# Head squares behind the scan's copies, and filter transform products ahead of the squares' sums

## The chip, the cores and the metric

The kernel runs on one core of a Trainium2 chip. The metric is the device time of one execution in microseconds (us). Engines are named as in the profile: PE is TensorE's matmul side and PEld its weight loads, DVE is VectorE, ACT is ScalarE, POOL is GpSimd, SP is SyncE. L1624 is line 1624 of the kernel before.

## The reference, cut to what matters

One inference step of a hybrid backbone on 128 context tokens and 512 latent tokens, width 1024, all in float32. Three pieces of it are touched: the filters of the long convolution, the modulated norm in front of the mixer, and the head norm and output projection at its end.

```python
def hyena_filters(seq_len, p):                 # for 128 and for 512 positions
    ...
    h = (h @ w3 + b3).reshape(seq_len, HY_ORDER, 2, HY_WIDTH)
    window = exp(-t * abs(decay)) + HY_MOD_SHIFT
    h = h * window
    h = h * rsqrt(sum(h * h, axis=(0, 2)) + EPS)       # squares summed over positions and directions
    ...

def mixer(xm, p, state, grid):
    proj = xm @ w_in                           # q, k, v, o, gates, three hyena parts
    h_f, (cf, nf, mf) = mlstm_scan(...)        # forward
    h_b, (cb, nb, mb) = mlstm_scan(...)        # backward
    h = h_f + rev(h_b)
    h = h * rsqrt(mean(h * h, axis=-1) + EPS)          # per head
    y_ml = h * head_gain * sigmoid(o)
    z = parts[-1]
    for n in range(HY_ORDER):
        z = parts[n] * long_conv(z, filt[n, 0], filt[n, 1], hy_bias[n])   # FFT of the filter
    return concatenate([y_ml, z]) @ w_out

h = rms_norm(x, g_norm) * (1 + sc) + sh        # sh, sc from silu(c) @ w_ada + b_ada
y = mixer(h, ...)
x = x + g1 * rms_norm(y, g)
x = x + g2 * rms_norm(hier_moe(rms_norm(x, g) * (1 + sc2) + sh2), g)      # 16 experts, top 2
```

## The kernel before

All of it is one program with an order written out by hand for every engine; the engines meet only through named counting semaphores. A helper `link` makes each VectorE or ScalarE operation bump a semaphore and wait for itself, so work on these engines runs strictly in the order written. A wait at the head of a queue holds everything behind it.

**Filters.** For each of two orders `o`, TensorE makes ten filter blocks (five 128-position tiles t, two directions s; w = 2t + s). ScalarE makes the window (`win`), VectorE multiplies it in (L973) into `ab`, ScalarE squares the block (`square`, L647), and VectorE turns the two directions of a tile into sum and difference (`combine`, L964 and L965). TensorE sums the squares over positions in three batches (`sum_squares`, L1596), the last behind block 9. Pieces of the modulation product (`ada_piece`, L1558) are strewn in between; each uses one 2 MB chunk of weights in a ring of three slots.

Then come ten transform products g per order (L1624, for g of 8 and 9 L1620): product 0 reads tile 1, product 1 tile 2, products 2 and 3 tiles 3 and 4. They go round four PSUM banks. ScalarE copies out products 0, 4, 5, 6, 8, 9 (`spectrum`, L655), VectorE adds out 1, 2, 3, 7 (L1000, L1001). Product 4 needs the bank of product 0, product 5 that of 1, product 7 that of 3. Between them lie: ScalarE's copy of the summed squares (L666), TensorE's lane sums (L1630), ScalarE's two square roots (L674), which need a table load, and on VectorE the bias rows (L984, L986: four operations of one row), which product 7 needs. In the second order TensorE also turns the first third of the modulation (`ada_turn(0)`, L1572) and does `ada_piece(7)` behind product 4.

**First norm.** ScalarE squares the five tiles of x (`x_square`, L622) in between, takes the root (L680), VectorE the reciprocal `xrs` (L994), and ScalarE scales the five tiles of `x_raw` in place (L686), between its copies of products 4, 5, 6. TensorE waits for all five and transposes x in ten bank-fuls (L1645), two in flight per evicting engine: even ones go to ScalarE (L699, L703), odd ones to VectorE (L1024, L1028), which apply `scaleA` and `mod` on the way to `hT`. Those two come from `ada_columns(0)` (L1013) and L1017, which VectorE does behind the cosine halves (L1003, L1004) of the second order. Then TensorE goes on with `ada_piece(8)` (L1558) and the projections.

**Scan.** Ten steps i, alternating direction. TensorE per step: half an output gate product (`out_gate_half`, L1803), the product with the state (L1848), with the values (L1856), and for the first eight the state update (L1864). ScalarE copies the state product out in four (L829) and, in odd steps, the output gate (`out_gate`, L783). VectorE adds the values' product to it (L1281). From step 7 on the first heads are normed: VectorE `heads_sum` (h_ready), ScalarE `heads_square` (L796), VectorE `heads_squares` (L1246), ScalarE `heads_root` (L800, with a table load), VectorE `heads_norm`.

**Output projection.** For each of five tiles j: `out_hyena` (L1888, 16 instructions per tile), `turn_heads` (TensorE L1873, VectorE L1301), `out_mlstm` (L1898, 16), then VectorE's `residual` into `x2` (L1314 to L1320) and TensorE's transposes of `x2` (L1908). The rows that `residual` needs and x itself are loaded by POOL when the last sum of the scan is done; `residual(0)` waits for x_sample.

**Experts.** Routing, then up to 70 groups of 32 token slots; the weights of expert e + 3 are loaded into the slots of expert e when its products are done.

Of the kernel before, what the change touches and what calls it, by code (L numbers as in the profile page):

```python
# [9 lines left out]
ALU = mybir.AluOpType  # L10
# [93 lines left out]
def emit(nc, a, stack):  # L104
# [491 lines left out]
    def _(act):  # L596
# [61 lines left out]
        for w in range(20):  # L658
            o = w // 10
            if w % 10 != 9:  # L660
                win(w + 1)
            square(w)
            if w % 10 == 9:
                act.wait_ge(S["sq_done"], 3 * o + 3)
                for i, rows in enumerate((P, 2 * LANE)):
                    link(A(lane_sums[i], ps[0:rows, 5 + i, :], ACT.Copy), "lanes_read")  # L666
                spectrum(o, 0)
                for t in ((0,), (2, 3))[o]:
                    x_square(t)
                act.wait_ge(S["norm_done"], o + 1)  # L670
                if o:
                    act.wait_ge(S["norm_stored"], 32)
                for i in range(2):
                    link(A(norm_rows[i], ps[0:1, 5 + i, :], ACT.Sqrt, bias=epsc[0:1, :]), "norm_sqrt")  # L674
                if o == 0:
                    win(w + 1)
                    x_square(1)
                else:
                    x_square(4)
                    link(A(xss, xss, ACT.Sqrt, bias=epsc, scale=1.0 / D), "x_rstd")  # L680
                for g in (4, 5, 6, 8, 9):
                    spectrum(o, g)
                    if o and g < 8:
                        act.wait_ge(S["xrs_ready"], 1)
                        for t in {4: (0, 1, 2), 5: (3,), 6: (4,)}[g]:
                            link(A(x_raw[:, t, :], x_raw[:, t, :], ACT.Copy, scale=xrs[:, t:t + 1]), "xn_ready")  # L686
            if w == 10:
                ada_row(0)
# [132 lines left out]
        for i in range(NSTEP):  # L821
# [3 lines left out]
            if t:  # L825
                act.wait_ge(S["inter_done"], i - 1)
                for h in range(H):
                    b, c = half4(h)
                    link(A(num[t][:, H * d + h, :], ps[:, 4 + b, c:c + DH + 1], ACT.Copy,  # L829
                           scale=qcols[:, t, 1, 32 * d + h:32 * d + h + 1]), "inter_read" if h == 3 else "act_chain")  # L830
            if i in (7, 8):
                heads_square(i - 7)

# [101 lines left out]
    def _(dve):  # L935
# [23 lines left out]
        link(CP(gate_pick[:, :, 32:32 + H], folded[:, 2:4, :]))  # L959

        def combine(o, t):

            dve.wait_ge(S["sq_ready"], 10 * o + 2 * t + 2)
            link(TT(ab[:, 1, t, :], ab[:, 1, t, :], ab[:, 0, t, :], ALU.subtract))  # L964
            link(STT(ab[:, 0, t, :], ab[:, 0, t, :], 2.0, ab[:, 1, t, :], ALU.mult, ALU.add),  # L965
                 "comb_done" if t == NT - 1 else "dve_chain")

        for o in range(ORD):
# [20 lines left out]
            for g in BY_VECTOR:  # L989
                if g == 3:  # L990
                    bias_rows_in()
                if o and g == 3:
                    dve.wait_ge(S["x_rstd"], 1)
                    link(dve.reciprocal(xrs, xss), "xrs_ready")  # L994
                n = 20 * o + 10 + g
                dve.wait_ge(S["filt_done"], n + 1)
# [4 lines left out]
                link(TT(h[:, old, :], new, h[:, old, :], ALU.subtract), "filt_read")  # L1001
            h = spec_h[:, o, 0]
            link(TT(h[:, 0:4:2, :], h[:, 0:4:2, :], h[:, 1:4:2, :], ALU.add))  # L1003
            link(STT(h[:, 1:4:2, :], h[:, 1:4:2, :], -2.0, h[:, 0:4:2, :], ALU.mult, ALU.add))  # L1004


        def ada_columns(third):

            dve.wait_ge(S["ada_t"], third + 1)
            lo = 16 * third  # L1010
            src = ps[:, ADA_BANK[third], :].rearrange("p (b j q) -> p j b q", b=4, j=4)[:, :, :, 0:2]
            bias = colsT[:, lo:lo + 16].rearrange("p (j b) -> p j b", j=4).unsqueeze(3).broadcast_to((P, 4, 4, 2))
            return link(TT(mod[:, lo:lo + 16, :].rearrange("p (j b) g -> p j b g", j=4), src, bias, ALU.add),  # L1013
                        "mod_ready")

        ada_columns(0)
        link(STT(scaleA, mod[:, 8:16, :], 1.0, colsT[:, 48:56].unsqueeze(2).broadcast_to((P, 8, 2)),  # L1017
                 ALU.add, ALU.mult), "modA_ready")
        for n in range(1, 10, 2):
# [73 lines left out]
        def context_products(o):  # L1093
# [10 lines left out]
            link(TT(xs, p[2], p[3], ALU.subtract), "mul_done")  # L1104

        dve.wait_ge(S["norm_cols"], 32)
        link(dve.reciprocal(norm_columns, norm_columns))
# [419 lines left out]
    def _(pe):  # L1527
# [72 lines left out]
        for o in range(ORD):  # L1600
            for w in range(10):
# [7 lines left out]
                if w in piece:  # L1609
                    ada_piece(4 * o + piece.index(w))  # L1610
            sum_squares(o, 2)
            pe.wait_ge(S["comb_done"], o + 1)
            pe.wait_ge(S["ld_dft"], 32)
            for g in range(10):
                n = 20 * o + 10 + g
                b = filter_bank(n)
                if g == 7:
# [8 lines left out]
                mm.then_inc(S["filt_done"], 1)  # L1626
                if g == 0:
                    pe.wait_ge(S["lanes_read"], 2 * o + 2)
# [8 lines left out]
        pe.wait_ge(S["spec_read"], 12)  # L1637
        pe.wait_ge(S["xn_ready"], NT)
        for n in range(10):
# [294 lines left out]
        out_hyena(0)  # L1934
        out_hyena(1)
        pe.wait_ge(S["st_ready"], LAST_UPD)
        turn_heads(0)
        out_mlstm(0)
        turn_heads(1)
        out_mlstm(1)  # L1940
# [118 lines left out]
```

## Time and profile before

| what | value |
|---|---|
| median of 3 runs | 868.31 us (863.45 to 868.75) |
| time of the profiled execution | 864.98 us |
| its span, first to last instruction | 862.1 us |
| mean granted TensorE clock | 0.967 |
| PE busy | 778.7 us (90%) |
| DVE, ACT, POOL busy | 49%, 33%, 13% |
| DMA | 191.40 MB, mean 222 GB/s |

```profile
PE   4998799999999999999998999799999989899920
PEclk9999999999999999989999999799999999999975
DMA  8978451132044402133009516969999999999145
```

The three strips cut the span in 40 equal slices of 21.55 us, with tenths of busy share, granted clock and DMA share. The filters fill the slices 2 to 5, the scan ends in slice 21, the experts run from slice 27 to 38.

### The profile page before, as it was taken

How to read it: one execution, taken by the hardware profiler on the slowest of the kernel's cores; microseconds unless marked ns; L12 is line 12 of the kernel's file. 1: busy time of each engine (PE TensorE's matmuls, PEld its weight loads, DVE VectorE, ACT ScalarE, POOL GpSimd, SP SyncE). 2: the span in 40 equal slices, each digit the busy share in tenths (PEclk: the TensorE clock that was granted, in tenths of full speed). 3: DMA queues.
4: the chain of work that ended last, by engine and by line, in shares of the span. 5: the costliest groups of instructions: out<-in, count | busy, mean ns of one | idle time of the engine just before them, and what ended most of it. 6: DMA issues, size and time to landing. Idle time of an engine off the chain costs nothing.

```text
span 862.1 us, 16880 instructions
## 1 busy us (share of the span) xinstructions
PE 778.7 (90%) x6727; PEld 448.2 (52%) x6727; DVE 419.9 (49%) x761; ACT 281.2 (33%) x559; POOL 108.5 (13%) x211
## 2 busy tenths in 40 slices
PE   4998799999999999999998999799999989899920
PEld 1232455554554457456664444357777667566610
DVE  5566713225881681754554675733343333243428
ACT  1667702113101201256222333223333333233315
POOL 4000100000001000001002000122222222122231
PEclk9999999999999999989999999799999999999975
DMA  8978451132044402133009516969999999999145
GB/s 246 411 300 341 134 195 36 63 114 82 18 178 165 132 1 99 25 123 123 0 22 367 202 44 221 397 244 418 416 420 416 419 418 420 419 415 393 61 150 233
DMA packets 40681, 191.40 MB, mean 222 GB/s; under 512 B 4641, under 2 KB 4937, under 8 KB 33010
## 3 DMA queue, kind: packets, MB, share of 16 engines
q1 hardware_dynamic: 29434, 155.12, 45.5%
q0 software_dynamic: 8640, 29.00, 9.9%
q10 hardware_dynamic: 2552, 6.50, 2.1%
q8 instruction: 41, 0.67, 0.3%
q14 instruction: 14, 0.11, 0.0%
HBM read 174.15 MB, written 16.45 MB: 221 GB/s over the span
## 4 chain that ended last, share of the span: by engine, by line
PE 73%; DMA 12%; DVE 7%; issue 3%; ACT 3%; SPq 1%; POOL 0%; POOLq 0%; DVEq 0%; ACTq 0%
PE banks L1654 16%; PE banks L2003 14%; DMA arena<-in_w_up 8%; PE banks L2014 6%; PE banks L1794 4%; PE banks L1655 4%; PE banks L1898 4%; PE banks L1888 4%; PE banks L1803 3%; DMA arena<-in_w_ada 3%; PE banks L1624 2%; PE banks L1686 2%; PE banks L1759 2%; PE banks L1558 2%; PE banks L1604 1%
## 5 line engine op out<-in xcount | busy, mean ns | idle before, releaser
L2003 PE MATMUL banks<-arena 128*32 128x256 f32 x3072 | 177.1, 382 | 9.0 <-DMA arena<-in_w_up 7.9
L1654 PE MATMUL banks<-arena 128*128 128x512 f32 x320 | 164.2, 595 | 1.5 <-issue 0.8
L2003 PEld LDWEIGHTS banks<-arena 128*32 128x32 f32 x3072 | 115.2, 111 | 63.0 <-issue 12.7
L1655 PEld LDWEIGHTS banks<-arena 128*128 128x128 f32 x320 | 60.8, 190 | 76.5 <-issue 76.5
L1480 DVE STREAM_TRANSPOSE arena<-arena 128x256 f32<-128x256 f32 x49 | 32.3, 659 | 135.3 <-PE banks L2003 130.1
L2014 PE MATMUL banks<-arena 128*32 128x256 f32 x1536 | 92.7, 379 | 1.2 <-DVE arena L1504 1.2
L2014 PEld LDWEIGHTS banks<-arena 128*32 128x32 f32 x1536 | 57.6, 110 | 26.7 <-DVE arena L1504 1.7
L1655 PE MATMUL banks<-arena 128*128 128x128 f32 x320 | 61.5, 274 | 0.0
L893 ACT ACTIVATE arena<-banks 32x256 f32<-32x256 f32 x98 | 36.7, 374 | 71.3 <-PE banks L2014 70.7
L1487 DVE COPY arena<-banks 32x256 f32<-32x256 f32 x98 | 41.4, 422 | 33.2 <-PE banks L2014 32.5
L1654 PEld LDWEIGHTS banks<-arena 128*128 128x128 f32 x320 | 48.5, 192 | 4.8 <-issue 3.3
L564 POOL DMA_INDIRECT arena<-expert_input,arena x47 | 46.3, 984 | 12.5 <-issue 12.5
L1042 DVE SCALAR_TENSOR_TENSOR arena<-banks,arena 128x504 f32<-128x504 f32 x12 | 8.9, 743 | 72.5 <-ACT arena L718 72.5
L912 ACT ACTIVATE arena<-banks 128x128 f32<-128x128 f32 x48 | 13.4, 278 | 92.1 <-PE banks L2003 92.1
L717 ACT ACTIVATE arena<-banks,arena 128x512 f32<-128x512 f32 x12 | 8.2, 687 | 97.9 <-PE banks L1655 97.9
L909 ACT ACT_TABLE_LOAD x24 | 30.8, 1283 | 28.6 <-DVE arena L1487 22.1
L1794 PE MATMUL banks<-arena 128*128 128x512 f32 x80 | 37.7, 633 | 0.0
L1888 PE MATMUL banks<-arena 128*128 128x512 f32 x80 | 35.1, 593 | 2.5 <-ACT arena L783 2.5
L1898 PE MATMUL banks<-arena 128*128 128x512 f32 x80 | 35.6, 598 | 1.7 <-DVE arena L1301 1.7
L1803 PE MATMUL banks<-arena 128*128 128x512 f32 x80 | 36.1, 594 | 0.0
L561 POOL COPY arena<-arena 128x1 int32 x47 | 8.5, 181 | 176.2 <-DVE arena L1480 176.2
L1794 PEld LDWEIGHTS banks<-arena 128*128 128x128 f32 x80 | 16.1, 204 | 20.2 <-issue 20.2
(378 smaller groups left out, 985.5 us busy)
## 6 DMA issues: line engine op xcount, KB each, us to landing
arena<-in_w_down SPq DMA_DIRECT2D x16, 2048.0 KB, 31.1
arena<-in_w_gate SPq DMA_DIRECT2D x15, 2048.0 KB, 26.7
arena<-in_w_up SPq DMA_DIRECT2D x15, 2048.0 KB, 31.7
arena<-in_w_ada SPq DMA_DIRECT2D x12, 2048.0 KB, 13.6
arena<-in_w_in SPq DMA_DIRECT2D x7, 2048.0 KB, 7.7
expert_output<-arena ACTq DMA_DIRECT2D x49, 128.0 KB, 6.5
expert_output<-arena POOLq DMA_DIRECT2D x1, 4096.0 KB, 20.4
arena<-in_w_out SPq DMA_DIRECT2D x2, 2048.0 KB, 7.9
```

The lines of the kernel that those rows point to most:

```text
L564: pool.indirect_dma_start(xr[n], None, h2_quarters, bass.IndirectOffsetOnAxis(ap=idx_now[n], axis=0))\
L893: ins = act.activation(ysb[n][:, l * 256:(l + 1) * 256], ps[l * LANE:(l + 1) * LANE, 5, 0:256], ACT.Copy)
L1480: dve.transpose(xg, xr[n].rearrange("p (r k) -> p k r", k=KD)).then_inc(S["xg_ready"], 1)
L1487: ins = dve.tensor_copy(ysb[n][:, l * 256:(l + 1) * 256], ps[l * LANE:(l + 1) * LANE, 5, 0:256])
L1654: M(ps[:, b, :], lhs, hT[:, k, CTX:TOK], start=k == 0, stop=k == KD - 1)
L1655: mm = M(ps[:, b + 1, 0:CTX], lhs, hT[:, k, 0:CTX], start=k == 0, stop=k == KD - 1)
L1794: mm = M(ps[:, 1 + n % 4, :], hT[:, k, n * P:(n + 1) * P], w[:, k, :], start=k == 0, stop=k == KD - 1)
L1803: mm = M(ps[:, 1, :], hT[:, k, t * P:(t + 1) * P], w[:, k, :], start=k == 0, stop=k == KD - 1)
L1888: M(ps[:, 1 + 2 * (j % 2) + c, :], part1t[:, k, t * P:(t + 1) * P], w[:, NB + k, :], start=k == 0, stop=False)
L1898: mm = M(ps[:, 1 + 2 * (j % 2) + c, :], ymlT[:, k, t * P:(t + 1) * P], w[:, k, :], start=False, stop=k == NB - 1)
L2003: mm = M(ps[q * LANE:(q + 1) * LANE, 2, 0:2 * P].rearrange("p (g a j) -> p g a j", g=2, j=LANE), xg[:, k, :], gate_up[e % 3][:, :, k, q, : ...
L2014: mm = M(ps[l * LANE:(l + 1) * LANE, 5, 0:256], aT[:, q * LANE:(q + 1) * LANE], downs[e % 3][:, q, l * 256:(l + 1) * 256], start=q == 0, s ...
```

## The change

Ahead of the last sum of squares of an order, TensorE now does transform products 0 and 1, each behind a `comb_done` of its own tile (`comb_done` now counts four per order). Product 2 follows the sum, and the lane sums follow product 2 (before: product 0). ScalarE copies product 0 before the summed squares. Of x's tiles ScalarE scales three (0, 1 behind product 4, 2 behind product 5); VectorE scales 3 and 4, ahead of its adds for product 7 of the second order, and right behind them does `ada_columns(0)` and `scaleA`. The cosine halves of the second order move behind VectorE's writes of `hT`. TensorE's wait ahead of the x transposes is for three scalings and for `modA_ready`. At the end of the scan `heads_square(0)` and `heads_square(1)` go one step back, behind the copies of steps 8 and 9, and TensorE does `turn_heads` 0 and 1 each behind one `out_hyena`, ahead of both `out_mlstm`.

```diff
@@ ScalarE, filters @@
             if w % 10 == 9:
+                spectrum(o, 0)
                 act.wait_ge(S["sq_done"], 3 * o + 3)
                 for i, rows in enumerate((P, 2 * LANE)):
                     link(A(lane_sums[i], ps[0:rows, 5 + i, :], ACT.Copy), "lanes_read")
-                spectrum(o, 0)
...
-                        for t in {4: (0, 1, 2), 5: (3,), 6: (4,)}[g]:
+                        for t in {4: (0, 1), 5: (2,), 6: ()}[g]:
@@ ScalarE, scan @@
-            if i in (7, 8):
-                heads_square(i - 7)
+            if i in (8, 9):
+                heads_square(i - 8)
@@ VectorE @@
-                 "comb_done" if t == NT - 1 else "dve_chain")
+                 "comb_done" if t else "dve_chain")
+        def cosine_halves(o):
+            h = spec_h[:, o, 0]
+            link(TT(h[:, 0:4:2, :], h[:, 0:4:2, :], h[:, 1:4:2, :], ALU.add))
+            link(STT(h[:, 1:4:2, :], h[:, 1:4:2, :], -2.0, h[:, 0:4:2, :], ALU.mult, ALU.add))
...
+                if o and g == 7:
+                    for t in (3, 4):
+                        link(TS(x_raw[:, t, :], x_raw[:, t, :], xrs[:, t:t + 1], None, ALU.mult))
+                    ada_columns(0)
+                    link(STT(scaleA, mod[:, 8:16, :], 1.0, colsT[:, 48:56].unsqueeze(2).broadcast_to((P, 8, 2)),
+                             ALU.add, ALU.mult), "modA_ready")
...
-            h = spec_h[:, o, 0]
-            link(TT(h[:, 0:4:2, :], ...))
-            link(STT(h[:, 1:4:2, :], ...))
-        ada_columns(0)
-        link(STT(scaleA, ...), "modA_ready")
+            if o == 0:
+                cosine_halves(o)
...
+        cosine_halves(1)
         dve.wait_ge(S["norm_cols"], 32)
@@ TensorE, filters @@
-            sum_squares(o, 2)
-            pe.wait_ge(S["comb_done"], o + 1)
             pe.wait_ge(S["ld_dft"], 32)
             for g in range(10):
                 n = 20 * o + 10 + g
+                if g == 2:
+                    sum_squares(o, 2)
+                if g < 3:
+                    pe.wait_ge(S["comb_done"], 4 * o + (1, 2, 4)[g])
...
-                if g == 0:
+                if g == 2:
                     pe.wait_ge(S["lanes_read"], 2 * o + 2)
...
-        pe.wait_ge(S["xn_ready"], NT)
+        pe.wait_ge(S["xn_ready"], 3)
+        pe.wait_ge(S["modA_ready"], 1)
@@ TensorE, output projection @@
         out_hyena(0)
-        out_hyena(1)
         pe.wait_ge(S["st_ready"], LAST_UPD)
         turn_heads(0)
+        out_hyena(1)
+        turn_heads(1)
         out_mlstm(0)
-        turn_heads(1)
         out_mlstm(1)
```

## Rows read from the trace of the kernel before

**Rows 1.** Busy time in stretches: length, engines busy (instructions), PEclk, DMA share, GB/s
```profile
450.90:478.20 27.30, 23.09 (x65) 10.87 (x65) 13.43 (x25) 6.89 (x15) 4.45 (x8) 1.00 0.96 364
...
380.00:385.00 5.00, 5.00 (x7) 1.89 (x6) 1.22 (x4) 4.64 (x12) 0.00 (x0) 0.50 0.00 0
...
580.00:800.00 220.00, 212.08 (x3888) 147.04 (x3881) 81.27 (x203) 71.31 (x162) 54.87 (x121) 0.99 1.00 413
```

**Rows 2.** Timeline, TensorE, filters: start, us, what, idle before and its releaser
```profile
42.89 1.06 PE L1596 MATMUL banks<-arena 128*32 128x512 f32 x8 [1.62 <-ACT arena L647]
...
45.08 1.13 PE L1624 MATMUL banks<-arena 128*128 128x512 f32 x2 [1.13 <-DVE arena L965]
...
46.14 1.97 PE L1630 MATMUL banks<-arena 128*1 128x512 f32 x4
...
48.03 9.83 PE L1624 MATMUL banks<-arena 128*128 128x512 f32 x22
...
80.32 1.13 PE L1624 MATMUL banks<-arena 128*128 128x512 f32 x2 [1.13 <-DVE arena L965]
```

**Rows 3.** Timeline, order 0: roots, bias rows, product 7's weight load; a later table load
```profile
48.19 1.28 ACT L674 ACT_TABLE_LOAD   x1
...
49.48 1.39 ACT L674 ACTIVATE arena<-banks,arena 1x512 f32<-1x512 f32 x2
...
52.42 1.39 DVE L984 TENSOR_TENSOR arena<-arena 1x512 f32<-1x512 f32 x2
...
56.74 0.30 PEld L1624 LDWEIGHTS banks<-arena 128*128 128x128 f32 x2 [0.68 <-DVE arena L1001]
...
547.67 1.28 ACT L882 ACT_TABLE_LOAD   x1 [6.45 <-DVE arena L1413]
```

**Rows 4.** Timeline, end of order 1, scaling and transposing of x
```profile
87.65 1.39 DVE L984 TENSOR_TENSOR arena<-arena 1x512 f32<-1x512 f32 x2
...
90.79 3.51 ACT L686 ACTIVATE arena<-arena 128x1024 f32<-128x1024 f32 x3 [0.55 <-DVE arena L994]
...
95.30 1.88 PE L1620 MATMUL banks<-arena 128*128 128x512 f32 x4
...
97.95 1.23 ACT L655 ACTIVATE arena<-banks 128x512 f32<-128x512 f32 x2
...
99.27 1.94 PE L1645 MATMUL banks<-arena 128*128 128x128 f32 x16 [2.09 <-ACT arena L655]
...
101.32 1.93 ACT L699 ACTIVATE arena<-banks,arena 128x128 f32<-128x128 f32 x4 [1.51 <-DVE arena L1017]
...
103.30 2.84 PE L1645 MATMUL banks<-arena 128*128 128x128 f32 x24 [2.09 <-ACT arena L699]
...
104.50 2.56 DVE L1028 TENSOR_SCALAR arena<-banks,arena 128x512 f32<-128x512 f32 x3 [0.64 <-PE banks L1645]
...
107.16 3.64 PE L1558 MATMUL banks<-arena 128*32 128x512 f32 x32 [1.02 <-ACT arena L703]
```

**Rows 5.** Timeline, end of the scan, output projection, first residual
```profile
444.61 1.05 PE L1848 MATMUL banks<-arena 128*128 128x129 f32 x8
...
446.70 0.63 ACT L796 ACTIVATE arena<-arena 128x512 f32<-128x512 f32 x1 [5.48 <-DVE arena L1242]
...
447.36 1.58 ACT L829 ACTIVATE arena<-banks,arena 128x129 f32<-128x129 f32 x4
...
454.29 13.97 PE L1888 MATMUL banks<-arena 128*128 128x512 f32 x32 [2.50 <-ACT arena L783]
...
469.55 7.13 PE L1898 MATMUL banks<-arena 128*128 128x512 f32 x16 [0.85 <-DVE arena L1301]
...
479.60 0.15 DVE L1314 TENSOR_SCALAR arena<-arena 128x1 f32<-128x1 f32 x1 [1.69 <-DMA arena<-in_x_sample]
...
482.75 0.69 DVE L1320 TENSOR_TENSOR arena<-arena 128x512 f32<-128x512 f32 x1
...
485.38 1.04 PE L1908 MATMUL banks<-arena 128*128 128x128 f32 x8
```

More of the change, by code:

```diff
@@ L959, in _, with ada_columns @@
         link(CP(gate_pick[:, :, 32:32 + H], folded[:, 2:4, :]))
+        def ada_columns(third):
+            dve.wait_ge(S["ada_t"], third + 1)
+            lo = 16 * third
+            src = ps[:, ADA_BANK[third], :].rearrange("p (b j q) -> p j b q", b=4, j=4)[:, :, :, 0:2]
+            bias = colsT[:, lo:lo + 16].rearrange("p (j b) -> p j b", j=4).unsqueeze(3).broadcast_to((P, 4, 4, 2))
+            return link(TT(mod[:, lo:lo + 16, :].rearrange("p (j b) g -> p j b g", j=4), src, bias, ALU.add),
+                        "mod_ready")
         def combine(o, t):
@@ L1001, in _ @@
                 link(TT(h[:, old, :], new, h[:, old, :], ALU.subtract), "filt_read")
-            h = spec_h[:, o, 0]
[L1003 to L1014, printed above, removed]
-        ada_columns(0)
-        link(STT(scaleA, mod[:, 8:16, :], 1.0, colsT[:, 48:56].unsqueeze(2).broadcast_to((P, 8, 2)),
-                 ALU.add, ALU.mult), "modA_ready")
+            if o == 0:
+                cosine_halves(o)
         for n in range(1, 10, 2):
```

## The prediction, made before the change was run

> **What bounds the kernel now.** I read the page first, for the shares, and then busy time by stretch: TensorE leads everywhere, as in the longest stretch shown, where it is busy for 212 of 220 us and no other engine for half of it [rows 1]. So only two kinds of time can be won: stretches in which TensorE stands still, and matmuls that run at half clock. Then I read the timeline of the two stretches that the diff touches.
>
> *Filters, first order.* TensorE is idle 1.62 us before the last squares' sum (it waits for ScalarE's last square) and 1.13 us before the first transform product (it waits for VectorE's last combine) [rows 2]. The second order repeats this. Behind it in the first stands a chain over three engines: lane sums, ScalarE's table load (1.28) and two roots (1.39), VectorE's four bias operations (one row of two, 1.39, stands for both), its adds for product 3, and then TensorE's product 7, which waited for those adds (its weight load starts at 56.74) [rows 3].
> *Between filters and the first projections.* TensorE starts the transposes of x at 99.27 after 2.09 us idle, starts the second batch at 103.30 after 2.09 more, and the modulation products at 107.16 [rows 4]. ScalarE carries this: five scalings of x at 1.16 us each, between copies of products at 0.60.
> *End of the scan.* ScalarE idles 5.48 us with heads_square(0) at the head of its queue, and only then does the four copies of step 8 (1.58); the same square sits ahead of step 9's copies. TensorE idles 2.50 us before the output projection, and 0.85 us twice, once behind each of the first two head transposes (the row of one is shown) [rows 5].
> From the projections to the scan, and in the expert stage, TensorE is close to gapless. In the expert stage the weight stream is full as well (DMA share 1.00 from 580 to 800), but its first load waits for expert 0's products, so the stream starts earlier if TensorE does [rows 1]. A gain ahead of it should pass through whole.
>
> **Part 1, order 0, on the clock of before.** TensorE is free at 42.89 - 1.62 = 41.27. Products 0 and 1 need only combines 1 and 2, which are long done. They are four instructions; a product instruction costs 0.43 (22 in 9.83, fill included) [rows 2], so they take 1.72 and end at 42.99: the squares' sum moves by 0.1 at most, and the combine still ends just before 45.08. There product 2 (four instructions) stands where product 0 (two) stood. Lane sums start at 46.14 + 0.86 = 47.00 and end at 48.97. Product 3 starts at 48.89 instead of 48.03 + 0.86 + 1.72 = 50.61, so TensorE is 1.72 ahead.
> But the lane sums end 0.86 later. Is the table load held by the wait? The load of line 882 stands behind 6.45 us of idling for VectorE [rows 3], so I take it that loads start after the wait. Then load 49.05, roots 50.34 to 51.73 (before: to 50.87). VectorE, which before only came to the bias rows at 52.42 because of its adds for product 2, is now free by 48.6 and waits for the roots: bias rows 51.77 to 54.58, adds for product 3 to 56.03, product 7 at 56.09 instead of 56.74. TensorE would have been there at 54.91. **0.65 of the 1.72 remains.** Bounds: 0, if another wait appears, and 1.72, if the roots are not late.
>
> **Order 1.** The same swap, still on the clock of before. Its product 0 started at 80.32, 35.24 after order 0's, so the lane sums end at 48.97 + 35.24 = 84.2, and load and roots at 86.95. Before, VectorE came to its bias rows at 87.65 [rows 4], later than the roots; now it comes at 87.0, so bias rows, x's reciprocal and ScalarE's scalings (90.79) are 0.65 sooner. ScalarE scales three tiles, not five: 2 x 1.18 = 2.36 less. Its last copy would end at 99.18 - 0.65 - 2.36 = 96.17, but product 9, with TensorE 1.72 ahead and no later wait, is on PSUM at 95.30 + 1.88 - 1.72 and a fill, 95.8, so this copy ends at 96.5. Transposes at 96.6 instead of 99.27: 2.67 won, with order 0's 0.65 **3.32**.
> VectorE now scales tiles 3 and 4 (two operations of 1024 elements, not in the trace: below by nothing, above by 2 x 0.69 each, the price per 512 elements of its adds [rows 3]; I take 0.7 to 1.4), then ada_columns and scaleA (0.2 each). All of it fits between the adds of product 3 (at 91.5) and those of product 7 (not before 95.0, ScalarE's copy of product 6); were the cover gone, it would cost up to 3.2. The modulation is then ready before the transposes. Before, ScalarE's first write of hT came at 101.32, 2.05 after the transposes began; now it needs only the first transposed bank, which by the row of the second batch (TensorE 103.30, VectorE's first write behind two banks at 104.50) is about 0.8: **1.26 more**. The rest up to 107.16 keeps its length [rows 4].
> The cosine halves (two operations, 2.5 us) move behind this, into VectorE's wait of 12 us for the first projection: nothing. The weight chunk for that projection is issued when modulation product 7 ends, and moves with it. Part 1: 3.32 + 1.26 = **4.6**.
>
> **Part 2, the scan's end.** Step 8's copies start when TensorE's product is there (445.7), not at 447.36. TensorE's own work in the scan ended at 454.29 - 2.50 = 451.79; two blocks of eight products (1.05 each) before that is the last output gate product, at about 450, so ScalarE's copy of it is done at 450.7, step 9's copies (behind the first of those blocks) at 452.6, and the second square follows them. The output projection's first half waits for the output gate (now 450.7) and its second for VectorE's last sum (453.4), so TensorE goes on at 451.64 instead of 454.29: **2.65**. The heads' chain (root with table load, norm 1.65) is ready at 456.6, ahead of the first half's end at 458.6; each transpose now has a projection of 7 us behind it, and both waits of 0.85 go: with the fills **1.85** [rows 5]. TensorE would reach the transposes of x2 4.5 ahead, at about 481.0.
> There something else is late: residual(0) waits for x_sample, released at 479.60. These loads go out on the last sum, 3.2 us sooner, but the queues were full from 450.9 to 478.2 but for 4% of 27.3 us [rows 1], and the first weights in them start as before. So it lands only 1.15 sooner. The second half of x2 is then ready at 482.75 + 0.69 - 1.15 = 482.3 against TensorE at 481.4: about 1.05 is given back. Part 2: 4.5 - 1.05 = **3.45**. VectorE's later residuals come 1.2 to 1.8 sooner, TensorE needs them 3.45 sooner, and they had 3.7 us to spare.
>
> **Sum:** 4.6 + 3.45 = 8.05. The profiled execution took 864.98 (span 862.1), the median is 868.31, 3.3 above. From the one I get 856.9, from the other 860.3; I predict the middle, 858.6.
>
> **Rivals.**
> *A: the roots are not late* (the table load runs ahead of the wait; line 882 speaks against it): 1.07 more in each order, 10.2 in all, 856.4. Chance 0.08.
> *B: the table switch costs more on the chain.* In these rows the root starts 0.01 after the load. If a switch after a wait took a second 1.28, both orders would lose it: 5.5 in all, 861.1. Chance 0.06. The Trainium skill (ScalarE: Activation LUTs, What ACT_TABLE_LOAD costs) puts a drain of 1.38 us beside the load's 1.28; by it the sum would be 8.05 - 2.76 = 5.3. The trace agrees on the load (1.28) and shows no drain behind it.
> *C: part 2 is eaten by x2.* x_sample lands no sooner, and TensorE waits for it a further 1.15: 6.9, 859.7. The full queues speak for it, the 4% of gaps against. Chance 0.12.
> *D: the clock moves.* From 380 to 385 the values' products ran at 0.50 (1.2 GHz), after a stretch of small transposes: 2.5 us lost, some 3 with the edges [rows 1]. If this fall goes, 855.5; if it doubles, 861.7. Nothing in the diff acts on it, but all of it shifts. Chance 0.17, both ways.
> *E: slower.* TensorE falls to 1.2 GHz among the x transposes (small products, as before 380) and stays there over the modulation products and first projections. An us at half clock loses 0.5, so it decides from 16 us on; at 18 us: 8.05 - 9 = 1 slower, 867.6. Before, this stretch had longer gaps and did not fall. Chance 0.02.
> The forecast itself: 0.55.
>
> **Numbers.** About 1% is what a measurement of this kernel can tell from no change. 8.05 is 0.93% of the profiled execution's time, so the forecast lies just inside that border and C further in: A, the good half of D and nearly half of the forecast (its terms are good to about 1 us) lie beyond it: faster 0.46, within 1% 0.51, slower 0.03. The three runs shown spread over 5.3 us, and that spread is wider than the rivals'; the range takes A and the good D below, B and the bad D above, from either base: 854.5 to 862.5.
>
> **What would show it.** Two more products between the last filter modulation product and the squares' sum in each order; product 7 still waiting for VectorE, some 1.2 us; the x transposes near 95.9 and the modulation products near 102.6; no gap of TensorE over 0.3 between scan and output projection, and one of about 1 us at the x2 transposes. I am wrong if VectorE's scalings take more than 1.7 each, if the table load starts ahead of the lane sums' end, or if the expert stage does not shift by the same 8 us.

## The result, and the profile after

| | before | after |
|---|---|---|
| median, us | 866.85 (863.45 to 868.75, 4 runs) | 854.34 (853.44 to 855.89, 4 runs) |
| ratio, 95% interval | 1 | 0.9865 (0.9842 to 0.9887) |
| profiled execution: time / span | 864.98 / 862.1 | 855.89 / 854.1 |
| mean granted clock | 0.967 | 0.967 |

The kernel became 1.35% faster, more than the 1% that a measurement can tell from no change. The forecast was 858.6; the measured 854.34 is 4.3 us under it and 0.16 under the low end of the range (854.5). The two profiled executions differ by 8.0 us in span and 9.1 in time, the medians by 12.5. The mechanisms are therefore read from the traces, and the difference between 8 and 12 is a question of its own.

In the changed kernel the line numbers have moved: the filter products are L1635, the lane sums L1641, the turns of the output projection L1885, its products L1900 and L1910, the transposes of x2 L1920.

**Filters, first order.** The timeline of the changed kernel, TensorE, then ScalarE, then VectorE (start, us, what, idle before and its releaser). Compare [rows 2, 3].

```profile
41.12 1.98 PE L1635 MATMUL banks<-arena 128*128 128x512 f32 x4
43.03 1.06 PE L1605 MATMUL banks<-arena 128*32 128x512 f32 x8
45.01 1.98 PE L1635 MATMUL banks<-arena 128*128 128x512 f32 x4 [0.91 <-DVE arena L974]
...
56.06 1.13 PE L1635 MATMUL banks<-arena 128*128 128x512 f32 x2 [0.97 <-DVE arena L1022]
...
48.97 1.28 ACT L674 ACT_TABLE_LOAD   x1 [2.34 <-PE banks L1641]
50.26 1.39 ACT L674 ACTIVATE arena<-banks,arena 1x512 f32<-1x512 f32 x2
...
51.74 1.39 DVE L999 TENSOR_TENSOR arena<-arena 1x512 f32<-1x512 f32 x2 [3.24 <-ACT arena L674]
53.17 1.40 DVE L1001 TENSOR_TENSOR arena<-arena 1x512 f32<-1x512 f32 x2
54.60 0.69 DVE L1021 TENSOR_TENSOR arena<-arena,banks 128x512 f32<-128x512 f32 x1
```

The first two products stand ahead of the squares' sums and fill the wait of 1.62; at product 2 TensorE still waits 0.91 for the last combine (before 1.13). The chain behind the lane sums then holds product 7: the table load waits for the lane sums (2.34 us idle ahead of it), the root starts 0.01 us behind the load, the four row operations follow, and TensorE waits 0.97.

**End of the second order.** The same timeline around the transposes of x (L1657) and the modulation products (L1567). Compare [rows 4].

```profile
90.88 1.54 DVE L1012 TENSOR_SCALAR arena<-arena 128x1024 f32<-128x1024 f32 x2
...
94.40 0.69 DVE L1021 TENSOR_TENSOR arena<-arena,banks 128x512 f32<-128x512 f32 x1 [1.53 <-ACT arena L655]
95.12 0.69 DVE L1022 TENSOR_TENSOR arena<-banks,arena 128x512 f32<-128x512 f32 x1
...
95.87 1.97 PE L1657 MATMUL banks<-arena 128*128 128x128 f32 x16 [1.08 <-DVE arena L1022]
...
96.64 1.93 ACT L699 ACTIVATE arena<-banks,arena 128x128 f32<-128x128 f32 x4 [0.15 <-PE banks L1657]
...
102.43 1.23 DVE L980 TENSOR_TENSOR arena<-arena 128x1024 f32<-128x1024 f32 x1
```

VectorE's two scalings take 0.77 each, TensorE transposes 3.40 us sooner, ScalarE writes hT 0.77 behind the transposes' start instead of 2.05. The modulation's products start at 102.49 (before: 107.16), and the cosine halves (from 102.43) lie behind VectorE's writes of hT. What TensorE waits for ahead of the transposes has changed, though: before it was ScalarE's last copy, now it is VectorE's second add for product 7, which ends at 95.81. ScalarE's last copy has ended at 95.53.

**End of the scan and output projection.** TensorE's timeline, then one row each of ScalarE and VectorE. Compare [rows 5].

```profile
444.42 1.06 PE L1868 MATMUL banks<-arena 128*128 128x129 f32 x8
445.31 7.03 PE L1900 MATMUL banks<-arena 128*128 128x512 f32 x16
452.18 0.60 PE L1885 MATMUL banks<-arena 128*128 128x128 f32 x4
452.62 7.03 PE L1900 MATMUL banks<-arena 128*128 128x512 f32 x16
459.49 0.60 PE L1885 MATMUL banks<-arena 128*128 128x128 f32 x4
459.93 13.90 PE L1910 MATMUL banks<-arena 128*128 128x512 f32 x32
473.66 0.60 PE L1885 MATMUL banks<-arena 128*128 128x128 f32 x4
474.77 0.66 PE L1920 MATMUL banks<-arena 128*128 128x128 f32 x4 [0.51 <-DVE arena L1329]
476.28 0.66 PE L1920 MATMUL banks<-arena 128*128 128x128 f32 x4 [0.85 <-DVE arena L1329]
476.77 7.03 PE L1900 MATMUL banks<-arena 128*128 128x512 f32 x16
...
439.46 1.57 ACT L829 ACTIVATE arena<-banks,arena 128x129 f32<-128x129 f32 x4 [4.54 <-PE banks L1860]
...
472.39 0.15 DVE L1323 TENSOR_SCALAR arena<-arena 128x1 f32<-128x1 f32 x1 [11.43 <-DMA arena<-in_x_sample]
```

ScalarE's copies of step 8 now wait for TensorE itself; TensorE enters the projection with no idle stretch; a turn is followed by its next product 0.44 us later. VectorE then waits 11.43 us for x_sample, and TensorE twice for VectorE.

**The clock in the values' products**, where TensorE fell to half clock in before [rows 1]. Busy time in a stretch, first before, then after (length, busy times, PEclk, DMA share, GB/s):

```profile
372.00:390.00 18.00, 18.00 (x70) 10.09 (x69) 7.16 (x6) 9.29 (x25) 0.00 (x0) 0.81 0.23 93
```

```profile
372.00:390.00 18.00, 18.00 (x76) 10.93 (x76) 7.96 (x10) 14.29 (x39) 0.00 (x0) 0.91 0.32 112
```

The loss is the length times what is missing from 1: 18 x 0.19 = 3.4 us before and, from the same stretch in pieces of 0.5 us, 1.7 after. So about 1.7 us of the trace's difference up to the scan's end are clock. TensorE's last block of the scan shows it: it starts 6.30 sooner (444.42, before 450.72), 1.63 more than the 4.67 of part 1. About as much is lost again by the end of the expert stage: what is 9.8 us sooner at expert 0's first product is 8.0 at the last. The largest piece lies behind a wait for w_up:

```profile
734.48 6.53 PE L2015 MATMUL banks<-arena 128*32 128x256 f32 x64 [3.66 <-DMA arena<-in_w_up]
```

These 64 products take 6.53 us, at half clock in part. In before they take 5.26, 1.27 less, behind a wait of 3.77, and in another execution of the changed kernel (e3 below) 5.35.

### The profile page after: what moved, and what is told of

It reads as the page before. It is cut to its first block, busy times and chain, and to the rows that moved or that the text cites. A ratio compares the mean times of both kernels' runs of the same rounds, so it can differ in the third digit from the quotient of the medians.

```text
span 854.1 us, 16884 instructions
## 1 busy us (share of the span) xinstructions
PE 778.4 (91%) x6727; PEld 446.5 (52%) x6727; DVE 421.2 (49%) x763; ACT 278.9 (33%) x557; POOL 108.9 (13%) x211
## 4 chain that ended last, share of the span: by engine, by line
PE 71%; DMA 14%; DVE 6%; issue 3%; ACT 3%; SPq 1%; POOL 1%; POOLq 0%; DVEq 0%; ACTq 0%
PE banks L1666 16%; PE banks L2015 14%; DMA arena<-in_w_up 8%; PE banks L2026 6%; PE banks L1806 4%; PE banks L1667 4%; PE banks L1815 4%; DMA arena<-in_w_ada 3%; PE banks L1910 2%; DMA arena<-in_x_sample 2%; PE banks L1900 2%; PE banks L1698 2%; PE banks L1771 2%; PE banks L1567 2%; PE banks L1613 1%
## 5 line engine op out<-in xcount | busy, mean ns | idle before, releaser
L1910 PE MATMUL banks<-arena 128*128 128x512 f32 x80 | 35.2, 595 | 0.0
L1900 PE MATMUL banks<-arena 128*128 128x512 f32 x80 | 35.2, 592 | 0.0
```

Of the source, the lines that this page charges most:

```text
L1900: M(ps[:, 1 + 2 * (j % 2) + c, :], part1t[:, k, t * P:(t + 1) * P], w[:, NB + k, :], start=k == 0, stop=False)
L1910: mm = M(ps[:, 1 + 2 * (j % 2) + c, :], ymlT[:, k, t * P:(t + 1) * P], w[:, k, :], start=False, stop=k == NB - 1)
```

## The experiments

All times stand beside the kernel before, run on the same chip. "Lost clock" below is (1 - mean granted clock) x span of a run. It includes the end of the program, which is at half clock from 830 us on in all 14 traces.

**The parts.** e1 keeps the scan and projection of before and takes part 1 of the diff; e2 the reverse; e3 is the changed kernel again.

> The filter and first-norm half of the change alone; end of the scan and order of the output projection as before. If the two halves are worth what the traces say (4.67 us from the filters, 2.7 + 2.3 - 1.8 from the scan's end), the modulation products start at 102.5 and this kernel is 4.7 us faster than before in its median. Rival: the median gain of about 12 comes from something in the first half that the trace does not show, then it is 8 or more faster here.

> The scan's end and the output projection's order alone. By the terms of the traces: TensorE enters the output projection 2.7 us sooner, both waits of 0.85 go, some 1.5 are given back at the transposes of x2; 3.2 to 3.5 us faster in all. Rival: 6 or more, if the halves of the 12 us in the medians lie here.

> The whole change once more, on the same chip and in the same rounds as its halves. If the 8.0 us between the two traces' spans are the real size, the ratio is 0.9905 to 0.991 (about 8 us); if the medians' 12 us are real, 0.986. It should be the sum of the two halves within 1 us, since neither touches what the other waits for.

| | median, us (before 864.79) | ratio, 95% | span |
|---|---|---|---|
| e1 part 1 | 859.24 | 0.9931 (0.9918 to 0.9944) | 857.1 |
| e2 part 2 | 861.16 | 0.9955 (0.9939 to 0.9971) | 859.8 |
| e3 whole | 852.28 | 0.9861 (0.9846 to 0.9876) | 850.7 |

By the ratios part 1 brings 6.0 us (predicted 4.6), part 2 3.9 (predicted 3.45), together 9.9; the whole brings 12.0. The difference of 2.1 is more than the 1 us that I had allowed. But the intervals are 1.1, 1.4 and 1.3 us wide to each side, which makes 2.2 for the difference, so it is not refuted that the parts add up. In e1's trace the modulation products start at 102.41, as in the whole, and TensorE idles 2.49 us before the projection, as in before:

```profile
447.83 14.38 PE L1900 MATMUL banks<-arena 128*128 128x512 f32 x29 [2.49 <-ACT arena L783]
```

**The halves of part 2.** e4 moves the squares only, e5 the turns only:

```diff
-            if i in (7, 8):
-                heads_square(i - 7)
+            if i in (8, 9):
+                heads_square(i - 8)
```

```diff
-        out_hyena(1)
         pe.wait_ge(S["st_ready"], LAST_UPD)
         turn_heads(0)
-        out_mlstm(0)
+        out_hyena(1)
         turn_heads(1)
+        out_mlstm(0)
         out_mlstm(1)
```

> Part 2 has two edits. This kernel makes one of them alone: the heads' squares move one block later in the scan (behind its last copies on ScalarE), the order of the output projection's turns stays that of before, and so does everything of part 1. My theory: the 2.5 us that TensorE waits ahead of the output projection's first matmul goes, so out_hyena(0) starts about 2.65 us sooner than in before; both 0.85 us waits between the first turn and its product and between the second turn and its product stay; the residual finds its input loaded and no stall stands ahead of the transposes of x2. About 2.65 us in all, 862.1 against 864.8. Rival (the squares' move and the turns' order pay only together): under 1 us here, because the projection then waits at its turns for what the squares used to cover.

> The other edit of part 2 alone: the output projection's order of turns and products is changed, the heads' squares stay where they were. My theory: TensorE still waits about 2.5 us ahead of the projection, the waits between a turn and its product (0.85 us twice) go, 1.7 to 1.85 us in all, 863.0 against 864.8; and since TensorE then comes to the second turn 1.8 us sooner rather than 4.5, the residual's wait for the load of x_sample is under 1 us and nothing is given back ahead of x2's transposes. With the squares alone the two then add up to 4.5 us, of which the whole part 2 keeps 2.7 to 3.9, the rest being the stall at x2. Rival: the turns' order is worth nothing, because the waits move to the heads' norm.

e4 took 862.20 (before 865.86; 0.9962, 0.9940 to 0.9983), e5 864.76 (0.9989, 0.9972 to 1.0007). Their medians were expected near 862.1 and 863.0. TensorE in e4 and then in e5:

```profile
452.19 1.06 PE L1856 MATMUL banks<-arena 128*128 128x129 f32 x8
453.08 13.90 PE L1888 MATMUL banks<-arena 128*128 128x512 f32 x32
466.81 0.60 PE L1873 MATMUL banks<-arena 128*128 128x128 f32 x4
468.27 7.13 PE L1898 MATMUL banks<-arena 128*128 128x512 f32 x16 [0.85 <-DVE arena L1301]
...
484.10 1.04 PE L1908 MATMUL banks<-arena 128*128 128x128 f32 x8
```

```profile
455.92 7.10 PE L1888 MATMUL banks<-arena 128*128 128x512 f32 x16 [2.50 <-ACT arena L783]
462.86 0.60 PE L1873 MATMUL banks<-arena 128*128 128x128 f32 x4
463.30 7.03 PE L1888 MATMUL banks<-arena 128*128 128x512 f32 x16
...
484.34 0.60 PE L1873 MATMUL banks<-arena 128*128 128x128 f32 x4
484.78 1.04 PE L1908 MATMUL banks<-arena 128*128 128x128 f32 x8
```

The two edits act each on its own waits, as the theory said. From the scan's last block to the projection e4 takes 0.89 us and before 3.57: 2.68. From the projection to the last turn e5 takes 28.42 and before 30.65: 2.23, more than the expected 1.7 to 1.85. In neither is there a wait at the transposes of x2: with one edit alone TensorE is not early enough to meet x_sample. The stall is a thing of both together, and that is why part 2 is worth less than 2.68 + 2.23. On time e5's interval includes 0, so its gain is shown by the trace only.

**The halves of part 1.** e6 is the swap of products and squares' sums, e7 the work dealt anew. The main lines of e6's edit and of e7's, each against the kernel before:

```diff
-            sum_squares(o, 2)
-            pe.wait_ge(S["comb_done"], o + 1)
...
+                if g == 2:
+                    sum_squares(o, 2)
+                if g < 3:
+                    pe.wait_ge(S["comb_done"], 4 * o + (1, 2, 4)[g])
```

```diff
+                if o and g == 7:
+                    for t in (3, 4):
+                        link(TS(x_raw[:, t, :], x_raw[:, t, :], xrs[:, t:t + 1], None, ALU.mult))
+                    ada_columns(0)
...
-        pe.wait_ge(S["xn_ready"], NT)
+        pe.wait_ge(S["xn_ready"], 3)
```

> Part 1 has two edits. This one alone: the first filter transform products of each order stand in front of the third block of the squares' sums, the work of VectorE and ScalarE around it is dealt as before. My theory: in each order product 7 still waits about 1 us for the add that frees its bank and keeps 0.65 us of 1.72; nothing is gained in the scaling or in the modulation. The transposes of x start near 97.9 us against 99.2 in before, the modulation's products near 105.9 against 107.2: 1.3 us in all, 863.5 against 864.8. Rival (the table load costs more once work is moved in front of it): under 0.5 us.

> The other edit of part 1 alone: two of five scalings move from ScalarE to VectorE, the modulation's first columns and the cosine halves are dealt anew, TensorE takes its first three blocks of x without waiting for all five; the filter products stay behind the squares' sums. My theory: transposes of x start near 98.2 us (1.0 sooner than before), the modulation's products about 1.3 us sooner still on top of it, near 104.8 against 107.2: about 2.4 us in all, 862.4 against 864.8. With the swap alone this makes 3.7 of the 4.7 us that both together moved the modulation's products; the missing 1 us would be what one edit opens for the other. Rival (the dealing only pays behind the swap): under 1 us here.

e6 took 863.34 (0.9969, 0.9951 to 0.9987), e7 861.84 (0.9966, 0.9938 to 0.9994). TensorE in e6, then in e7:

```profile
56.24 1.12 PE L1626 MATMUL banks<-arena 128*128 128x512 f32 x2 [0.97 <-DVE arena L1001]
...
98.17 2.15 PE L1647 MATMUL banks<-arena 128*128 128x128 f32 x9 [3.17 <-ACT arena L655]
```

```profile
97.85 1.94 PE L1655 MATMUL banks<-arena 128*128 128x128 f32 x16 [0.79 <-DVE arena L1022]
```

The swap alone starts the transposes 1.10 us sooner; 3.17 us of idle time stand ahead of them, since ScalarE's scalings hold them. Its modulation products were expected near 105.9 and start at 106.99. But here TensorE was at half clock from 97.3 to 104.2 (PEclk 0.66 from 96 to 106), among the transposes themselves, so their row says nothing on the rest. The dealing alone starts the transposes 1.42 sooner and the modulation products at 104.44, 2.72 sooner. 1.10 + 2.72 = 3.82 of the 4.67 of both. I put the missing 0.85 down to what each opens for the other: the swap makes TensorE early for the transposes, which only pays when ScalarE is early too. No run separates this. Both rivals are out: e6 gains 1.10 at the transposes and 2.7 by its ratio (the rival said under 0.5), e7 2.72 at the modulation products and 2.9 by its ratio (the rival said under 1), though on time alone e7's interval, 0.5 to 5.4, would not exclude it.

**What is still given back.** e8 lets residual(0) go without x_sample. It is the residual of the x_prompt tile and reads nothing of x_sample; residual(1), the next, still waits for it. (The expectation calls the two "halves".) e9 puts order 0's row operations behind the adds of product 3. e10 does both, e11 is the changed kernel beside them, and e12 repeats e10. The main lines of e8's edit, and that of e9:

```diff
-        pool.dma_start(x2[:, 0, :], xp_t).then_inc(S["ld_x2"], 16)
+        pool.dma_start(x2[:, 0, :], xp_t).then_inc(S["ld_rowctx"], 16)
...
-                dve.wait_ge(S["ld_rowctx"], 48)
-                dve.wait_ge(S["ld_x2"], 32)
+                dve.wait_ge(S["ld_rowctx"], 64)
...
+                dve.wait_ge(S["ld_x2"], 16)
```

```diff
-                if g == 3:
+                if g == (3 if o else 7):
```

> The changed kernel with one edit: the residual's first half, which reads only x_prompt and the projection, no longer waits for the load of x_sample (x_prompt counts on another semaphore), its second half still does. In the changed kernel this residual waits 11.43 us on that load and the transposes of x2 behind it make TensorE idle 0.51 and 0.85 us; the second half of the projection was there 1.80 us less early than TensorE's entry and turns had gained. My theory: the stall was the one term of my sum that was too small (1.80 instead of 1.05), and it goes: from the second turn to out_hyena(2) TensorE takes 1.3 to 1.8 us less, about 852.5 against a changed kernel at 853.6 to 854.3. Rival 1: the stall is hidden behind something else (the norm of x2 or the routing, both behind the second half, end no sooner), 0 to 0.3 us. Rival 2: the load of x_sample itself is late for other reasons, so that the second half's residual then makes TensorE wait at its own transposes for as long: 0 us, with an idle stretch of over 1 us ahead of those.

> The changed kernel with one edit: in order 0 the two rows of reciprocals and biases (1.42 us each on VectorE, behind the roots) stand behind the adds of product 3 rather than in front of them. In the changed kernel TensorE waits 0.97 us at product 7 for the add that frees its bank, which is queued behind these two. My theory: product 7 starts at the end of product 6, 0.9 us sooner, and all behind it up to the scan moves by 0.9 us. Rival: the copies that read the rows then come late and TensorE waits at product 9 or at order 1's first products for as long (0 us).

> Both edits on top of the changed kernel: x_prompt's residual alone and order 0's rows behind the adds. They lie some 370 us apart and share no engine's queue, so they should add up: 2.2 to 2.7 us less than the changed kernel of the same chip, about 851.5. If either is worth nothing, 0.9 to 1.8.

> The changed kernel unchanged, on the same chip as the three above, so that they are compared with it and not with the kernel before. Theory: 11 to 12 us under the kernel before (0.9865 so far), of which 8 are the sum of the steps and 1 to 2 are a difference in how often TensorE's clock is granted at half; the granted clock times the span should give a loss of about 27 us here against 30 in the kernel before. Rival: the excess over 8 us belongs to the change itself, and the loss is the same in both.

> The kernel with both edits a second time. Two questions. (1) Is it really faster than the changed kernel? Its own times of the first run (852.45 against 855.24 on the same chip) and its trace (out_hyena(2) 4.1 us sooner, of which 1.6 are a shorter stretch at half clock) say 2 to 2.7 us; the ratio to the kernel before should again be 0.984 to 0.987. Rival: as the changed kernel, 0.988. (2) Is the stretch at half clock in the values' products of 374 to 388 us a matter of chance alone? In the four executions traced so far that have part 1 as before it lost 3.4, 3.4, 3.4 and 1.7 us (before, the two halves of part 2 and part 2 whole), in the nine with part 1 changed, whole or half, 1.7 four times or nothing five times. If the change really made it shorter, this trace shows 0 or 1.7 us lost there; if it is chance alone, 3.4 is about as likely.

| | median, us (before) | ratio, 95% | span |
|---|---|---|---|
| e8 | 853.00 (865.40) | 0.9864 (0.9842 to 0.9885) | 849.4 |
| e9 | 855.27 (865.40) | 0.9890 (0.9868 to 0.9912) | 849.3 |
| e10 | 852.45 (865.40) | 0.9859 (0.9837 to 0.9881) | 847.8 |
| e11 | 855.24 (865.40) | 0.9877 (0.9853 to 0.9901) | 853.9 |
| e12 | 852.63 (864.94) | 0.9851 (0.9823 to 0.9878) | 850.1 |

TensorE in e8, from the last turn on; then TensorE and VectorE in e9, product 7 and what it waits for:

```profile
472.03 0.60 PE L1885 MATMUL banks<-arena 128*128 128x128 f32 x4
472.46 1.04 PE L1920 MATMUL banks<-arena 128*128 128x128 f32 x8
473.34 1.02 PE L1900 MATMUL banks<-arena 128*128 128x512 f32 x2
```

```profile
55.11 1.10 PE L1635 MATMUL banks<-arena 128*128 128x512 f32 x2 [0.22 <-DVE arena L1001]
...
50.70 0.69 DVE L1021 TENSOR_TENSOR arena<-arena,banks 128x512 f32<-128x512 f32 x1 [2.39 <-PE banks L1635]
51.42 0.69 DVE L1022 TENSOR_TENSOR arena<-banks,arena 128x512 f32<-128x512 f32 x1
52.14 1.39 DVE L999 TENSOR_TENSOR arena<-arena 1x512 f32<-1x512 f32 x2
```

In e8 the stall is gone: 1.31 us from turn to out_hyena(2) instead of 3.11, so 1.80 won, and no other wait in its place. That refutes e8's second rival in the trace. From the turn to expert 0's first product e8 takes 79.33 us and after 80.81, with as much lost to the clock in both (6.8 us between 528 and 556), so 1.5 of the 1.8 arrive at the experts, and the first rival (0 to 0.3) is out too. On time e8 is 2.2 under e11, but the intervals of the two ratios overlap. In e9 product 7 starts 0.95 sooner and the modulation products at 101.52 instead of 102.49: it arrives whole, and its rival is out. On time e9 alone shows nothing: 855.27 beside 855.24 in e11. An edit of 0.9 us is less than the spread of its runs (852.04 to 857.33), and I don't call it a gain in time.

Both edits together: ten runs of e10 and e12 have a mean of 852.47, the 14 of the changed kernel (its own four, e3, e11) 854.14. The difference is 1.7 with an interval of 0.4 to 2.9; the traces say 1.5 + 0.95, and 2.2 to 2.7 was expected (it is 2.8 beside e11). The interval leaves out 0, but the runs come from several chips; beside e11 alone the intervals of the ratios overlap. Of the versions tried it has the lowest median, by about 0.2% against the changed kernel; e8 alone lies within 0.6 us of it.

**The clock, across the traces.** The stretch from 372 to 390 us in e10 and in e12, which are the same kernel:

```profile
372.00:390.00 18.00, 17.94 (x74) 10.70 (x75) 9.37 (x12) 15.80 (x41) 0.00 (x0) 1.00 0.34 117
```

```profile
372.00:390.00 18.00, 18.00 (x62) 10.73 (x62) 6.49 (x9) 12.85 (x34) 0.00 (x0) 0.81 0.25 86
```

Nothing was lost in the one and 3.4 us in the other, and out_hyena(0) starts 3.8 us apart, at 442.65 and at 446.42. So one execution of a kernel can differ from another by nearly half of what this whole change brings. In all 14 traces this stretch lost nothing, 1.7 or 3.4 us. With part 1 as before (before, e2, e4, e5) the losses were 3.4, 1.7, 3.4 and 3.4; with part 1 changed, whole or half, 1.7 in after, e1, e3 and e11, nothing in e6 to e10, 3.4 in e12. The means are 3.0 and 1.0. But e12 was to tell the two theories apart and came out with the value that I had given to chance. That the change itself shortens the stretch is therefore not shown. e11 speaks no clearer: expected were 11 to 12 us under before and a lost clock of 27 against 30, measured 10.2 and means of 28.3 against 29.7.

## Why the prediction was right, and where it wasn't

| step | predicted | measured in the traces |
|---|---|---|
| product 7 of order 0 | 56.09, waiting 1.2 | 56.06, waiting 0.97 |
| transposes of x | 95.9 | 95.87 |
| modulation products (part 1) | 102.6 (4.6) | 102.49 (4.67) |
| VectorE's scaling, each | 0.7 to 1.4 | 0.77 |
| entry into the output projection | 2.65 | 2.68 |
| its two turns | 1.85 | 2.30 |
| given back at x2 | 1.05 | 1.80 |
| part 2 | 3.45 | 3.18 |

**Part 1** went as worked out but for one step. The prediction has the transposes of x wait for ScalarE's last copy, and they wait for VectorE's second add for product 7 (95.81, the copy ends at 95.53). Its own times made this nearly a tie: two adds of 0.72 behind a copy at 95.0 end at 96.45, ScalarE's last copy at 96.5. So the start came within 0.1 us, in part by luck, and by these rows a faster ScalarE at its last two copies would win nothing there. That 0.65 of 1.72 remains in order 0 follows from the chain behind the lane sums: the products came early, but the roots wait for lane sums that end 0.86 later, and the four row operations stand ahead of the adds that free product 7's bank. e9 takes exactly this away and gets 0.95. Rival A (the table load runs ahead of the wait) is out: the load starts at 48.97, behind the lane sums (48.88). Rival B is out too: the root starts at 50.26, 0.01 behind the load. The Trainium skill (ScalarE: Activation LUTs, What ACT_TABLE_LOAD costs) puts a drain of 1.38 us beside the load's 1.28. The trace agrees on the 1.28, and neither of the two loads ahead of the roots shows a drain between it and its root (48.97 and 50.26, 83.59 and 84.89).

**Part 2** had the right mechanism and two terms of wrong size. The turns were worth 2.30: from a turn to its product took 1.46 before and 0.44 now, twice 1.02 with the fills, and the remaining 0.26 lies in the groups of products, which take 0.07 to 0.10 longer behind a wait (13.97 and 7.13) than without one (13.90 and 7.03). I had counted 1.85 for all of it. The stall at x2 was worth 1.80: 0.48 because TensorE came that much earlier than I had it (4.98 for 4.5), 0.24 because the row that waits for x_sample moved 0.91 and not 1.15 beyond the common shift. (The prediction's 1.05 is itself 0.15 more than the difference of its two times, 482.3 and 481.4.) The two errors, 0.45 and 0.75, cancel in part, which is luck. Rival C (x_sample lands no sooner) was nearer than I thought, but 0.91 is not 0. e4 and e5 show that the stall needs both edits, e8 that residual(0) makes it, which never needed x_sample.

**The sum**, 4.67 + 2.68 + 2.30 - 1.80 = 7.85 from the rows, against 8.05. The span's difference of 8.0 looks like a confirmation of this, but that is in part luck: it holds 1.6 of clock won in the values' products and about as much lost behind.

**What failed is the step from the sum to the time.** Three things in it:

- The base. I took 866.65, the middle between the profiled execution and a median of three runs. The 62 runs of the kernel before that came with the experiments have a median of 865.4. That is 1.2 of the 4.3.
- The size. Over all runs the change is worth 11.2 us (mean of 62 against mean of 14, interval 10.2 to 12.2), not 8: the other 3.1. Both repeats came out above 8, by the medians 12.5 in e3 and 10.2 in e11. Per run the lost clock has a mean of 29.7 us before and 27.6 after, 2.0 less (0.9 to 3.2). Within each kernel, over 148 runs in all, an us of lost clock goes with 0.40 us of time; at equal lost clock by that slope the change is worth 10.4 (9.6 to 11.2), part 1 5.0 (3.7 to 6.2), part 2 3.6 (2.5 to 4.8). Where a loss lies in the values' products it costs TensorE all of it, and the difference of means there, 3.0 - 1.0, has just the size of the 2.0; by that, 8 + 2 = 10 and about 1 is left. This is rival D's better half, to which I gave less than 0.17. But the place rests on 14 traces, against which e12 speaks, so the cause of these 2 to 3 us stays open. In the profiled execution they don't come from a wait that I missed, since the rows add up to its 8.0. The clock's part is of the right size, but it isn't shown that the change makes it.
- The range. By its own words it takes A, B and both halves of D "from either base". From 864.98 the good half of D gives 853.8, from 868.31 the bad half 863.4; the stated 854.5 to 862.5 is narrower at both ends. The measured 854.34 lies in what the words describe and 0.16 outside the stated figure.

The chances had "faster by over 1%" at 0.46 and "within 1%" at 0.51. The forecast lay so near the border that either could come; the measured interval (1.13% to 1.58% faster) is beyond it. Rival E did not come: between 94 and 300 us the changed kernel's clock is 1.00 throughout. Its first half did come in two other traces: in e2, where this part is as before, and in e6 the clock fell around the start of the x transposes (PEclk 0.83 and 0.66 from 96 to 106). It was back at full before the modulation products in both. The expert stage did not shift by one figure, as the prediction asked (9.8 us at expert 0's first product, 8.0 at the stage's last); 1.27 of the 1.8 between is the half clock behind the wait for w_up.

## What to carry to other kernels

- Work moved into a gap pays only until the next chain that starts later because of it. Follow the chain of the displaced work (here lane sums, table load, roots, rows, adds) to the next wait before a gain is written down, and look then whether an operation in it can step back behind the one that is waited for.
- Two edits on one path can be additive in their own waits and still share a stall behind them. A load that lands in time for each alone is late for both together; ask of every wait on two loads whether what stands behind it reads both.
- A trace is one execution. Compare the granted clock of each stretch in several before a difference of 2 us is put down to the change, and take the base from many runs.

## What the runs showed of the hardware

- Half clock (1.2 GHz) differs from one execution to the next of one kernel. In the values' products it starts 2 to 4.5 us behind the first of the gates' small products (40 columns and fewer; 3.0 in before, 4.4 in after), although TensorE is busy throughout (18.00 of 18.00 us in before). The same instructions ran 6.8 us at half clock in e12 and none in e10.
- In e1 a fall also lay between 445 and 454, at the output projection's start behind the 2.49 us idle (PEclk 0.88 from 445 to 459). At the wait of 3.7 us for w_up, between 730 and 748, it came in 13 of the 14 traces. In e12 the same wait (3.78 us) is followed by 64 products in 3.66 us, with PEclk 1.00. At the 2.50 us idle ahead of the projection the clock stayed at 1.00 in before and e5. No run here separates what a wait does from chance.
- In after, ScalarE's table load is held by the wait of its own activation: 2.34 us idle until the lane sums end, load, root 0.01 us behind.
- VectorE multiplies 128x1024 by a value per row in 0.77 us, while its addition of two tensors of that size (L980) takes 1.23. I had bounded the first by the second's rate (2 x 0.69) above. The Trainium skill (VectorE: DVE Perf Modes, The perf-mode tier table) has fp32 operations on one tensor in SBUF at double rate and on two tensors at single rate; the two rows agree.
